# Query norm applied as the exponential's scale, norm weights folded into k, k's sum of squares by one wide product

## The reference

```python
q = rms_norm(q.reshape(B, S, N_HEADS, 2, HEAD_DIM), q_g) * (HEAD_DIM ** -0.5)
k = rms_norm(k.reshape(B, S, N_HEADS, 2, HEAD_DIM), k_g)
...
for start in range(0, S, Q_BLOCK):          # Q_BLOCK = 128: 4 blocks
    s = jnp.einsum("bhcqd,bhckd->bhcqk", qb, kb).astype(jnp.float32)
    p = jax.nn.softmax(jnp.where(mask, s, -jnp.inf), axis=-1)   # block-causal
    a = p[:, :, 0] - lam * p[:, :, 1]
    outs.append(jnp.einsum("bhqk,bhkd->bhqd", a.astype(vb.dtype), vb))
o = rms_norm(o, subln_g) * (1.0 - lambda_init)
return o @ w_o
```

## Time and profile before

| what | us |
|---|---|
| median of 3 runs (lowest, highest) | 1824.3 (1820.43, 1833.15) |
| span of the profiled execution | 1827.1 |
| PE busy in it | 1444.1 (79%) |
| DVE, ACT, POOL busy in it | 525.7, 328.0, 297.9 |
| attention stage in it (from first q product to last output projection) | 927 to 1264 |

### The profile page before, as it was taken

How to read it: one execution, slowest core, us unless ns; L and a number is a source line. 1 busy time by engine, 2 the same in 40 slices (tenths; PEclk the granted TensorE clock), 3 DMA queues, 4 the chain that set the end, 5 groups by cost and what they waited for, 6 DMA issues and landing times.

```text
span 1827.1 us, 16973 instructions
## 1 busy us (share of the span) xinstructions
PE 1444.1 (79%) x6028; PEld 650.3 (36%) x6028; DVE 525.7 (29%) x858; ACT 328.0 (18%) x629; POOL 297.9 (16%) x381
## 2 busy tenths in 40 slices
PE   5966239788887878878589999988797778888784
PEld 3422114433232222223256766745232222222231
DVE  1999981221110111011133433332310111011112
ACT  2433331100000000000133444331010000000000
POOL 0666630012111111111000000000121111111100
PEclk9988659789898998989889999998898899899887
DMA  9110200478999999999760210303789999999995
GB/s 324 35 69 0 92 1 23 185 304 323 400 373 411 405 403 397 409 393 401 302 232 1 79 61 1 122 40 128 317 330 401 399 409 397 407 399 387 396 405 196
DMA packets 91250, 473.13 MB, mean 259 GB/s; under 512 B 19676, under 2 KB 19676, under 8 KB 40261
## 3 DMA queue, kind: packets, MB, share of 16 engines
q1 hardware_dynamic: 78500, 443.12, 60.5%
q0 software_dynamic: 10400, 16.82, 2.5%
q10 hardware_dynamic: 2304, 12.58, 1.8%
HBM read 466.43 MB, written 23.33 MB: 268 GB/s over the span
## 4 chain that ended last, share of the span: by engine, by line
PE 52%; DMA 25%; DVE 15%; SPq 4%; issue 3%; ACT 1%; POOL 0%; ACTq 0%; POOLq 0%; DVEq 0%
DMA ring<-in_moe_w 22%; PE banks L1252 17%; PE banks L1269 8%; PE banks L1361 6%; DVE area L844 5%; PE banks L1201 5%; DVE scratch L844 4%; PE banks L1394 3%; SPq L317 3%; PE banks L1242 1%; PE banks L1260 1%; PE banks L1455 1%; PE banks L1408 1%; PE banks L1435 1%; DMA area<-y_dram 1%
## 5 line engine op out<-in xcount | busy, mean ns | idle before, releaser
L1252 PE MATMUL banks<-ring,scratch 128*64 128x512 f32 x2016 | 510.3, 665 | 171.4 <-DMA ring<-in_moe_w 161.4
L1252 PEld LDWEIGHTS banks<-ring,scratch 128*64 128x64 f32 x2016 | 159.2, 153 | 518.9 <-issue 517.8
L986 DVE COPY scratch<-banks 128x256 f32<-128x256 f32 x65 | 27.6, 424 | 820.9 <-PE banks L1260 820.9
L1269 PE MATMUL banks<-ring,scratch 128*64 128x512 f32 x976 | 226.3, 606 | 3.0 <-DVE scratch L986 3.0
L661 ACT ACTIVATE scratch<-banks 64x512 f32<-64x512 f32 x65 | 38.3, 589 | 633.4 <-PE banks L1252 633.4
L496 POOL TENSOR_TENSOR scratch<-scratch 128x512 f32<-128x512 f32 x88 | 131.9, 1499 | 105.8 <-ACT scratch L633 93.8
L1150 PE MATMUL banks<-hT,ring 128*128 128x512 f32 x256 | 121.8, 640 | 29.9 <-DVE scratch L826 29.2
L514 POOL COPY at_out<-rows_out 128x1 int32 (+1 forms) x64 | 11.7, 183 | 749.2 <-ACT scratch L665 749.2
L1361 PE MATMUL banks<-hT,ring 128*128 128x512 f32 x256 | 120.1, 614 | 0.8 <-DVE hT L803 0.8
L1269 PEld LDWEIGHTS banks<-ring,scratch 128*64 128x64 f32 x976 | 66.8, 138 | 116.3 <-issue 109.5
L1201 PE MATMUL banks<-ring,area 128*128 128x512 f32 x200 | 99.6, 652 | 10.5 <-ACT area L643 9.4
(11 more groups left out here) (208 smaller groups left out, 1219.3 us busy)
## 6 DMA issues: line engine op xcount, KB each, us to landing
ring<-in_moe_w SPq DMA_DIRECT2D x374, 1024.0 KB, 11.4
area<-in_moe_w SPq DMA_DIRECT2D x12, 1024.0 KB, 14.6
ring<-in_attn_w_qkv SPq DMA_DIRECT2D x12, 1024.0 KB, 14.2
ring<-in_conv_w_in SPq DMA_DIRECT2D x8, 1024.0 KB, 13.7
area<-y_dram ACTq DMA_DIRECT2D x8, 1024.0 KB, 8.0
ring<-in_conv_w_out SPq DMA_DIRECT2D x4, 1024.0 KB, 13.3
xn_dram<-area ACTq DMA_DIRECT2D x8, 512.0 KB, 2.6
hT<-in_moe_w SPq DMA_DIRECT2D x4, 1024.0 KB, 12.3
```

Source lines behind the costliest of these rows:

```text
L1252: last = mm(bank[2 + s][q * SLOTS:(q + 1) * SLOTS, :], xeT[s][:, j, h, :], w[:, c, :], start=c == 0, stop=c == NC - 1)
L1269: last = mm(bank[6 + s][q * SLOTS:(q + 1) * SLOTS, :], hidT[s][:, j, :], w2c[:, j, q * 512:(q + 1) * 512], start=j == 0, stop=j == 3)
```

## The change

The queries are no longer normed ahead of the scores. ACT copies the raw q into qT (L717 of the changed kernel); scores are taken with raw q and normed k. The inverse root of a query's mean square is a number per token, so per partition of the scores, and goes in as the exponential's scale (q_rs); the negated maximum is multiplied by it (mx_scaled), one more DVE instruction per block. Both weights and the factor 1/8 are multiplied into k's weight once. The sum of squares of q is taken as before (q_squares, one group of 4 products). That of k is one product with the block of ones as the stationary operand (k_squares, 128 x 512): it gives every partition of its half the sum, in the layout of k, in the whole of bank 4. ACT takes the root of 128 x 512 (k_std), DVE inverts 128 x 512 (k_rs) and one instruction makes kT from bank 3. The scaled copies, the spreading and the transpositions (L1104, L1382) are gone. Bank 4 is shared by both sums; k_squares waits for q_root.

```diff
-        qk_rs_wide = [area1[:, (4 + c) * T:(5 + c) * T] for c in range(2)]
-        qk_g_sb = [area1[:, (2 + c) * T:(3 + c) * T] for c in range(2)]
+        k_rs = area1[:, 4 * T:5 * T]
+        k_std = area1[:, 2 * T:3 * T]
...
-        ss_bank = bank[4][:, 0:4 * NT]
-        rs_bank = [bank[4], bank[1]]
+        q_ss_bank = bank[4][:, 0:2 * NT]
+        k_ss_bank = bank[4]
...
             def qk_square(h, c):
                 act.wait_ge(qk_ready, 2 * h + c + 1)
                 a.activation(qk_sqb[c], qk_bank[c][:], ACT.Square).then_inc(qk_sq, 1)
-                if h >= 1:
-                    act.wait_ge(qk_done, 2 * h - 1 + c)
-                a.activation(qk_g_sb[c], qk_bank[c][:], ACT.Copy, scale=qk_g[:, c:c + 1]).then_inc(qk_scaled, 1)
+                if c == 0:
+                    a.activation(qT[h % 2], qk_bank[0][:], ACT.Copy).then_inc(q_copied, 1)
...
                 for c in range(2):
-                    a.activation(p_sb[i % 3][:, c, 0:W], score[:, c, 0:W], ACT.Exp, bias=mx[:, i, c:c + 1],
+                    a.activation(p_sb[i % 3][:, c, 0:W], score[:, c, 0:W], ACT.Exp, bias=mx_scaled[:, i % 4, c:c + 1],
+                                 scale=q_rs[h % 2][:, 2 * b + c:2 * b + c + 1],
                                  accum_out=ps[:, i, c:c + 1]).then_inc(p_done, 1)
...
                 if h is not None:
-                    act.wait_ge(qk_ss, 2 * (h + 1))
-                    a.activation(qk_std, ss_bank, ACT.Sqrt, bias=eps[:], scale=1.0 / HEAD_DIM).then_inc(qk_root, 1)
+                    act.wait_ge(q_ss, h + 1)
+                    a.activation(q_std, q_ss_bank, ACT.Sqrt, bias=eps[:], scale=1.0 / HEAD_DIM).then_inc(q_root, 1)
+                    act.wait_ge(k_ss, h + 1)
+                    a.activation(k_std, k_ss_bank[:], ACT.Sqrt, bias=eps[:], scale=1.0 / HEAD_DIM).then_inc(k_root, 1)
...
-            link(v.tensor_scalar(qk_g[:, 0:1], qk_g[:, 0:1], HEAD_DIM ** -0.5, None, ALU.mult))
+            link(v.tensor_scalar(qk_g[:, 1:2], qk_g[:, 1:2], qk_g[:, 0:1], HEAD_DIM ** -0.5, ALU.mult, ALU.mult))
...
             def maxima(i):
-                W = P * (pairs[i][1] + 1)
+                h, b = pairs[i]
+                W = P * (b + 1)
                 dve.wait_ge(s_ready, i + 1)
-                v.tensor_reduce(mx[:, i, :], score[:, :, 0:W], AX.X, ALU.max, negate=True).then_inc(m_done, 1)
+                link(v.tensor_reduce(mx[:, i, :], score[:, :, 0:W], AX.X, ALU.max, negate=True))
+                v.tensor_tensor(mx_scaled[:, i % 4, :], mx[:, i, :], q_rs[h % 2][:, 2 * b:2 * b + 2], ALU.mult).then_inc(m_done, 1)
...
-            def norm_qk(h, c):
-                dve.wait_ge(qk_rs_ready, 2 * h + c + 1)
-                v.tensor_tensor((qT, kT)[c][h % 2], qk_g_sb[c], rs_bank[c][:], ALU.mult).then_inc(qk_done, 1)
+            def scale_q(h):
+                dve.wait_ge(q_root, h + 1)
+                v.reciprocal(q_rs[h % 2], q_std).then_inc(q_rs_done, 1)
+
+            def norm_k(h):
+                dve.wait_ge(k_root, h + 1)
+                link(v.reciprocal(k_rs, k_std))
+                v.scalar_tensor_tensor(kT[h % 2], qk_bank[1][:], qk_g[:, 1:2], k_rs, ALU.mult, ALU.mult).then_inc(k_done, 1)
...
                 if h is not None:
-                    dve.wait_ge(qk_root, h + 1)
-                    link(v.reciprocal(qk_rs, qk_std))
-                    for c in range(2):
-                        v.tensor_copy(qk_rs_wide[c].rearrange("p (k f) -> p k f", f=HEAD_DIM),
-                                      qk_rs[:, 2 * NT * c:2 * NT * (c + 1)].unsqueeze(2).to_broadcast([P, 2 * NT, HEAD_DIM])
-                                      ).then_inc(qk_rec, 1)
+                    scale_q(h)
                 if e is not None:
                     dve.wait_ge(on_std, e + 1)
                     cols = slice(NT * e, NT * (e + 1))
@@ -1111,11 +1116,9 @@
                     v.tensor_tensor(oh[e % 2], oh[e % 2], o_rn[:, cols].unsqueeze(2).to_broadcast([P, NT, P]),
                                     ALU.mult).then_inc(on_done, 1)
                 if h is not None:
-                    norm_qk(h, 0)
+                    norm_k(h)
                 if g is not None:
                     take_o(i + 3)
-                if h is not None:
-                    norm_qk(h, 1)
...
                 if half == 0:
                     loaded(pe, u)
                     if h >= 1:
-                        pe.wait_ge(qk_scaled, 2 * h - 1 + c)
+                        pe.wait_ge((q_copied, k_done)[c], h)
...
-            def sum_squares(h, c):
-
-                pe.wait_ge(qk_sq, 2 * h + c + 1)
-                if c == 0 and h >= 1:
-                    pe.wait_ge(qk_done, 2 * h - 1)
+            def q_squares(h):
+
+                pe.wait_ge(qk_sq, 2 * h + 1)
+                if h >= 1:
+                    pe.wait_ge(k_done, h)
                 for t in range(NT):
-                    k = 2 * (NT * c + t)
-                    last = mm(ss_bank[:, k:k + 2], qk_sqb[c][:, t * P:(t + 1) * P], halves[:, 0:HEAD_DIM + 1:HEAD_DIM],
+                    last = mm(q_ss_bank[:, 2 * t:2 * t + 2], qk_sqb[0][:, t * P:(t + 1) * P], halves[:, 0:HEAD_DIM + 1:HEAD_DIM],
                               start=True, stop=True)
-                last.then_inc(qk_ss, 1)
-
-            def spread_rs(h, c):
-
-                pe.wait_ge(qk_rec, 2 * h + c + 1)
-                if c == 1 and h >= 1:
-                    pe.wait_ge(p_done, 2 * NT * h)
-                for t in range(NT):
-                    last = mm(rs_bank[c][:, t * P:(t + 1) * P], qk_rs_wide[c][:, t * P:(t + 1) * P], ident[:], start=True, stop=True)
-                last.then_inc(qk_rs_ready, 1)
+                last.then_inc(q_ss, 1)
+
+            def k_squares(h):
+
+                pe.wait_ge(qk_sq, 2 * h + 2)
+                pe.wait_ge(q_root, h + 1)
+                mm(k_ss_bank[:], halves[:], qk_sqb[1], start=True, stop=True).then_inc(k_ss, 1)
...
                 h, b = pairs[i]
                 W = P * (b + 1)
                 if b == 0:
-                    pe.wait_ge(qk_done, 2 * (h + 1))
+                    pe.wait_ge(q_copied, h + 1)
+                    pe.wait_ge(k_done, h + 1)
...
                 if h is not None:
                     qk_half(h, 1, 0)
-                    sum_squares(h, 0)
+                    q_squares(h)
...
                 if h is not None:
-                    sum_squares(h, 1)
+                    k_squares(h)
                     v_half(h, 0)
-                if h is not None:
-                    spread_rs(h, 0)
-                    spread_rs(h, 1)
```

More of the change, by code:

```diff
@@ L150, in trunk @@
             sem("picks_done"), sem("ranks_ready"), sem("hot_done"), sem("lists_ready"), sem("lists_done"))
-        qk_ready, qk_sq, qk_ss, qk_root, qk_rec, qk_rs_ready, qk_scaled, qk_done = (
-            sem("qk_ready"), sem("qk_sq"), sem("qk_ss"), sem("qk_root"), sem("qk_rec"), sem("qk_rs_ready"),
-            sem("qk_scaled"), sem("qk_done"))
+        qk_ready, qk_sq, q_ss, k_ss, q_copied, q_root, k_root, q_rs_done, k_done = (
+            sem("qk_ready"), sem("qk_sq"), sem("q_ss"), sem("k_ss"), sem("q_copied"), sem("q_root"), sem("k_root"),
+            sem("q_rs_done"), sem("k_done"))
         v_ready, v_done = sem("v_ready"), sem("v_done")
@@ L285, in trunk @@
         o_std = scratch[:, 5312:5312 + 32]
+        mx_scaled = scratch[:, 5560:5560 + 8].rearrange("p (i c) -> p i c", c=2)
+        q_std = scratch[:, 5552:5552 + 2 * NT]
         o_r = scratch[:, 5344:5344 + 32]
@@ L288, in trunk @@
         o_junk = scratch[:, 5408:5408 + P]
-        qk_std = scratch[:, 5536:5536 + 4 * NT]
-        qk_rs = scratch[:, 5552:5552 + 4 * NT]
+        q_rs = [scratch[:, 5536 + 2 * NT * b:5536 + 2 * NT * (b + 1)] for b in range(2)]
         ahead = (0, 4)
```

## The result

The changed kernel takes 1838.0 us in the median of 20 runs (1830.56 to 1842.8), the kernel before 1826.9 in 20 runs (1820.04 to 1836.09). The ratio is 1.0053, 95% interval 1.0037 to 1.0069: slower by 7 to 13 us, and by 11.1 from median to median. That is a small loss, half a per cent, but the interval is clear of no change. Run again beside other versions, on another occasion, the changed kernel gave 1.0074 (1.0048 to 1.01), 14.0 us from median to median.

A forecast was written before the change was run, and what follows sets the result against it. PE was taken to bound attention, with the whole tail moving with attention's end. Waits less removed work (+9.5 us) and clock falls (+4.2) gave +13.7 on a median of 1824.3: 1838.0, range 1827 to 1849.

The forecast's parts named there:

- PE's steps are the stage's pace: Attention steps 2 to 7: PE is always busy, so a microsecond of its work removed or wait added is one of the stage.
- 2.61 us less per head, k_squares 0.97: PE, each head: narrow products (0.82) and eight transpositions (1.79) go, k_squares adds 0.97, so 1.64 us shorter without waits.
- k_squares 3.07 late: PE, each full step: k_squares waits 2.62 us for q's root on ACT, plus 0.45 put ahead of that wait.
- the 0.09 for the first weight load of the transpositions: PE, fourth block: transpositions that start after a wait show their weight load, 0.09 us, part of the 0.45 ahead of the wait.
- No drain behind the table load: ACT, before q's root: the table load costs 1.28 us and no drain follows it, so nothing is added.
- The rival of the page: ACT's table switch: a drain of about 1.38 us is paid in each of eight waits, +11 us, 1849; chance 0.03.
- Steps +1.43, step 1 +1.2, step 0 -0.3: +9.5: Attention without clock falls: steps 2 to 7 each 1.43 us longer, step 1 1.2 longer, step 0 0.3 shorter; in all +9.5.
- k's norm is covered by 3.6 us: Before the next scores: k's longer norm ends 3.6 us early, costing nothing; rival that it becomes the wait, 1846 or more, 0.05.
- The clock, 2.5 falls and 4.2 us: PE's clock after the new pauses in eight steps: 2.5 falls at 1.7 us each, +4.2 us, ends 0 and 13.6.
- the count: Expert-stage pauses of 2.0 to 3.0 us: 7 of 11 brought a clock fall; for attention, 5 of 8 steps, +8.7 us.
- The tail moves with attention: Expert stages: most loads wait for attention's output projection, so each microsecond of attention counts as one of the span.
- the rival in which the experts' loads swallow the delay: Expert stages: loads start by their own clock, so the delay vanishes, 1824 to 1829; chance 0.12.

The follow-up runs named there:

- e3: Changed kernel with three unused products of 384 columns (2.0 us of PE work) ahead of k_squares' wait; ratio 1.0033.
- e6: Changed kernel with q's norm left out of the softmax (no scale operand, no product on the maxima), root and its wait kept; ratio 1.0064.
- e2: Kernel before with one wait added: v's first half waits for the root of both sums; 1843.4 us, ratio 1.0095.
- e4: Changed kernel with k_squares moved behind v's first half on PE, bank still shared and wait kept; 1813.4 us, ratio 0.9926.
- e5: Changed kernel with k's inversion of 512 columns done three times over instead of once; 1877.1 us, ratio 1.0292.
- e1: Changed kernel with q's sums in bank 2, so that k_squares no longer waits for q's root; 1811.3 us, ratio 0.992.
- e7: Changed kernel with q's sums in bank 2 and k_squares ahead of the fourth block's transpositions on PE; 1809.9 us, ratio 0.9928.
- e11: Changed kernel with the three unused products in the pause, run again beside the changed kernel on one chip; ratio 1.003.
- e8: Changed kernel with one unused product of 512 columns ahead of k_squares' wait; ratio 1.004.

## Why the prediction was right

The forecast was 1838.0 with a range of 1827 to 1849; 1838.0 was measured, and the mechanism was that of the forecast. That the two times are equal is luck. The forecast adds 13.7 us to the 1824.3 of three runs; in 20 runs the kernel before has 1826.9, and the change costs 11.1 (7 to 13), 14.0 on the other occasion. The base was 2.6 us too low and the difference as much too high.

- *PE's steps are the stage's pace.* Right. Every microsecond of wait lengthened its step, and e3's unused work inside the pause lengthened none.
- *2.61 us less per head, k_squares 0.97.* Right: it takes 0.94. The rest of the step is another 0.07 shorter than the removal says (8.57 from v's start to the next scores, where 8.64 were worked out). The difference is in v's first half, 3.57 us to the next piece instead of 3.65; why is not shown.
- *k_squares 3.07 late.* Measured 3.08, in part by luck. The exponential of 512 columns with the second operand takes 772 ns against 683, 0.089 where 0.085 were taken; the chained product on the maxima takes 0.16 and puts the exponential 0.19 later, where 0.20 were taken; combine ends 0.38 later, where 0.37 were taken, and e6 takes the same 0.38 away. But the 0.09 for the first weight load of the transpositions is not there: they take 0.66 as before, and take_aT is 0.38 late and not 0.45. That is also why e6 gained 0.38 and not 0.45. And k_squares begins 0.14 after the root's end, where 0.04 were taken. The two errors, each about 0.1, cancel. That the kernel before has the same wait under cover is shown by e2, that the cover decides by e4.
- *No drain behind the table load.* Right: in the changed kernel the root starts 1.30 us after the load's start, and the load itself 0.01 after the end of take_aT. The rival of the page, 1.38 us more in each wait, fell.
- *Steps +1.43, step 1 +1.2, step 0 -0.3: +9.5.* Measured without falls +1.33, +1.15 (e3) and -0.2: +9.0. Step 0 is taken from the start of k's last projection half to the first scores, 14.39 before and 14.21 after. The 0.10 that a step is shorter than the forecast are the 0.03 of k_squares and the 0.07 of v above. Step 8, costed at nothing, has 30.01 us before and 30.07 after, from its first scores to the last piece of output_ahead.
- *k's norm is covered by 3.6 us.* Measured 3.5 in the timeline and 3.4 by e5; in step 0, which the forecast didn't look at, 2.2. That rival fell. Its price didn't fit its own condition: an inversion twice as long adds 3.35 us, which a cover of 3.6 still hides, so it would have cost about nothing and not 8 us.
- *The clock, 2.5 falls and 4.2 us.* This was the chosen number, between none and the count. Two profiled executions have three falls and 6.0 us each. They are not drawn at random: the same steps in both. The price of 1.7 held for two of the three; the third cost 2.86, since its low stretch lasted longer. So the term was undersized, 4.2 for 6.0, and the attention stage's steps are 15.0 us longer in all, above the 13.7. The runs agree on its size: filling the pause gave 4, 8 and 9 us in three pairs by the ratios, around the 6.0 of the steps.
- *The tail moves with attention.* Right within a few us; the rival in which the experts' loads swallow the delay fell, since in e1, e4 and e7 the gain arrives at the end too (13 to 15 us by the ratios, 10 to 13 by the steps), and so does the loss of e5 (53 by both) and of e2 (17 by both). In the profiled pair alone 15.0 us of the steps have become 7.7 of the span. What stays open: nearly all versions with the changed attention are better in the ratio than in their steps, the changed kernel by 5 and by 1.5 us on its two occasions, the filled ones by 2 to 3.5, e1 and e4 by 3 to 4, e7 not at all. The stretch behind attention with its two lengths may be a part of it, and no run tells.

## What to carry to other kernels

Before a transposition or a copy is taken away from the busiest engine, look what its neighbours were hiding: here 13 us of removed work turned into a loss because the wait for a root moved from behind 3.6 us of products to ahead of them. When two results share a bank, the second producer waits for the first one's reader, so ask when that reader runs in its own queue; another bank, or one swap of two lines, made the same change a gain of 0.7 to 0.8%. And a pause on PE has a second price in the clock, to be counted with it.

## What the runs showed of the hardware

- A repeated pause of 2.5 us on PE brought the clock to 1.2 GHz in three steps of seven, one of 0.6 us (e3, e11) in none. At 1.7 us it was none of seven in e8 and two of seven in e2, so the length of the pause isn't all. In the expert stages of the kernel before it was 7 of 11 for pauses of 2.0 to 3.0 us and none for shorter ones.
- The falls repeat with the program: steps 1, 4 and 5 in both executions of the changed kernel; in e5 steps 1, 2, 4 and 6. Making a step 0.38 us shorter (e6) moved the falls to steps 1, 2, 4 and 7; their cost stayed, 6.2 us for 6.0.
- Unused products in a pause cost nothing as long as they end before it does: with 2.0 us of them (e3) or 1.0 (e8) the steps keep their 34.00 us.
- DVE's inversion of 128 x 512 takes 3.35 us, 4.5 times a product with two operands of the same size (0.75), in all eight places as in the one row before.
- The wait is there because both sums lie in one bank. The Trainium skill, page "PSUM — Partial Sum Buffer", section "PSUM bank collisions raise a hardware error", says that two engines in the same bank and the same 32 partitions at one time raise an error, at different columns too. No run here shows it, and a version without order between the two was not tried.
